# A depthwise convolution with silu, moved from the fused scan stage into the input projection

## What is computed

```
u = x @ W_in  -> [q | k | v | forget logits | z | xBC | dt | gate_att | gate_ssm]

def causal_conv(xbc, buf, w, b):
    xp = jnp.concatenate([buf.astype(xbc.dtype), xbc], axis=1)
    y = b
    for j in range(CONV_WIDTH):
        y = y + w[j] * xp[:, j:j + l]
    return jax.nn.silu(y), xp[:, l:]

def mamba_branch(z, xbc, ...):
    xbc, new_buf = causal_conv(xbc, conv_buf, conv_w, conv_b)
    xs, bm, cm = jnp.split(xbc, [D_SSM, D_SSM + SSM_GROUPS * SSM_STATE], axis=-1)
    ...                                    # chunked scan over xs, bm, cm; gate by silu(z); grouped norm
```

## Time and profile before

| | |
|---|---|
| median of 3 runs | 5410.88 us (5408.63 to 5411.28) |
| profiled execution | 5412.87 us, its span 5411.1 us |
| TensorE / VectorE / ScalarE / GpSimd busy in the span | 75% / 61% / 16% / 27% |
| projection | 0 to 1476 us, TensorE at its full clock |
| fused stage, groups 0 to 6 | 1532 to 2114 us |
| fused stage, last group | 2114 to 2192 us |
| merge and experts | 2192 to 5411 us |

### The profile page before, as it was taken

One profiled execution on the slowest core, in us unless ns is written; L12 is line 12 of the kernel. 1 busy time (PEld: TensorE's weight loads), 2 busy tenths in 40 slices (PEclk: granted clock), 3 DMA queues, 4 the chain that ended last, 5 costly groups with the idle time before them and its releaser, 6 DMA issues. The chain is left out here.

```text
span 5411.1 us, 60657 instructions
## 1 busy us (share of the span) xinstructions
PE 4053.6 (75%) x24165; PEld 3236.8 (60%) x24165; DVE 3325.7 (61%) x4454; ACT 849.1 (16%) x1210; POOL 1463.3 (27%) x1609
## 2 busy tenths in 40 slices
PE   9999999999957777899999999999999900000000
PEld 7999999999935545798798555555555500000000
DVE  2322222222257766433452897878879789999998
ACT  2212221212112222322352000000000000000000
POOL 0000000000043333000010122222222367777774
PEclk9999999999967777899999999999999955555555
DMA  4332323232177876534564999999999999999998
GB/s 156 117 126 100 106 100 105 100 106 100 57 254 271 289 278 241 196 110 169 173 211 161 355 419 419 398 418 421 421 420 419 421 379 410 410 410 409 410 410 331
DMA packets 336652, 1462.02 MB, mean 270 GB/s; under 512 B 84452, under 2 KB 113028, under 8 KB 196600
## 3 DMA queue, kind: packets, MB, share of 16 engines
q0 software_dynamic: 174304, 995.20, 46.1%
q1 hardware_dynamic: 131304, 430.86, 22.0%
q10 hardware_dynamic: 30768, 32.11, 1.8%
HBM read 1362.71 MB, written 94.75 MB: 269 GB/s over the span
## 5 line engine op out<-in xcount | busy, mean ns | idle before, releaser
L2231 DVE SCALAR_TENSOR_TENSOR i_acc<-i_row,i_cf,i_acc 128x2048 f32<-128x2048 f32 x571 | 1344.8, 2355 | 156.1 <-DMA i_row<-in_expert_v,i_ei 119.3
L2038 PE MATMUL i_p_h<-i_xT,i_ut 128*128 128x384 f32 x4096 | 1322.4, 486 | 0.0
L2038 PEld LDWEIGHTS i_p_h<-i_xT,i_ut 128*128 128x128 f32 x4096 | 779.1, 190 | 540.9 <-issue 0.6
L2347 POOL DMA_INDIRECT i_row<-in_expert_v,i_ei x576 | 544.9, 946 | 633.7 <-DVE i_acc L2231 512.2
L246 PE MATMUL a_acc<-a_xh,a_wh 128*128 128x288 f32 x3104 | 672.2, 298 | 18.1 <-DVE a_xl L466 13.4
L246 PE MATMUL a_acc<-a_xh,a_wl 128*128 128x288 f32 x3104 | 665.2, 296 | 0.0
L246 PE MATMUL a_acc<-a_xl,a_wh 128*128 128x288 f32 x3104 | 664.8, 296 | 0.0
L246 PEld LDWEIGHTS a_acc<-a_xh,a_wh 128*128 128x128 f32 x3104 | 499.2, 189 | 29.6 <-issue 26.0
L2222 DVE CUSTOM_DVE_ANT_0 i_row<-i_row,i_acc 128x2048 f32<-128x2048 f32 x192 | 433.5, 2286 | 125.1 <-DMA i_row<-in_expert_u,i_ei 123.3
L246 PEld LDWEIGHTS a_acc<-a_xl,a_wh 128*128 128x128 f32 x3104 | 500.4, 189 | 0.0
L246 PEld LDWEIGHTS a_acc<-a_xh,a_wl 128*128 128x128 f32 x3104 | 500.3, 189 | 0.0
(11 more groups left out here) (310 smaller groups left out, 5450.9 us busy)
## 6 DMA issues: line engine op xcount, KB each, us to landing
i_ut<-in_u_tiles SPq DMA_DIRECT2D x128, 1024.0 KB, 9.7
a_w<-in_w_in SPq DMA_DIRECT2D x97, 1024.0 KB, 4.8
f_w<-in_w_out SPq DMA_DIRECT2D x32, 1024.0 KB, 5.1
f_w<-in_w_query SPq DMA_DIRECT2D x32, 1024.0 KB, 5.2
tmp_uT<-a_out POOLq DMA_DIRECT2D x97, 288.0 KB, 2.4
tmp_Ha<-i_ho ACTq DMA_DIRECT2D x128, 192.0 KB, 9.2
f_w<-in_w_bs SPq DMA_DIRECT2D x16, 1024.0 KB, 4.9
c_csb<-tmp_cs SPq DMA_DIRECT2D x32, 288.0 KB, 5.8
```

Of the source, the lines that this page charges most:

```text
L2038: last = nc.tensor.matmul(p_h[:, e % 2, 0:ND], ut[:, e % RU, k * P:(k + 1) * P], xT[:, k, :], start=(k == 0), stop=(k == KT - 1))
L2231: v.scalar_tensor_tensor(acc, row[:, m % R, :], cf[:, j, k:k + 1], acc, ALU.mult, ALU.add).then_inc(row_used, 1)
L2347: pool.indirect_dma_start(row[:, m % R, :], None, table, bass.IndirectOffsetOnAxis(index, axis=0)).then_inc(row_in[m % R], 16)
```

## The change

The convolution and its silu are done in the projection, on the tile that was just evicted. The tiles get new places in `uT`: in each round of 20 slots, the 8 slots with t % 5 in (1, 3) compute tiles of `xBC`, the 12 others those of z and the gates. In a convolution slot VectorE runs `conv` right behind its eviction: 4 small copies and 8 arithmetic instructions, the same shapes as before. ScalarE does the silu in the slot after, in front of its eviction. GpSimd doesn't store the raw tile; it stores the finished one as `xcT` and the new convolution state (27 columns) as `convT`. SyncE loads the channels' taps, bias and old state (29 columns) along with each such tile's weights. The fused stage loads the finished tiles into `xc2`, and its edges, convolution and silu are gone.

```
--- before.py
+++ after.py
+    CONV = [t for t in range(SLOTS) if t % 5 in (1, 3)]
+    PLAIN = [t for t in range(SLOTS) if t % 5 not in (1, 3)]
...
+                    if t in CONV:
+                        c = CONV.index(t)
+                        if type(r) is not int or c >= 4:
+                            sp.wait_ge(conv_sum, 8 * r + c - 3)
+                        sp.dma_start(cp[:, c % 4, :], io["conv_par"][ds(8 * r + c, 1)].rearrange("a p n -> (a p) n")
+                                     ).then_inc(cp_in[c % 4], 16)
...
+                def silu(r, c):
+                    act.wait_ge(conv_sum, 8 * r + c + 1)
+                    nc.scalar.activation(cv[:, c % 2, :], cv[:, c % 2, :], ACT.Silu).then_inc(conv_out, 1)
...
+                    if t - 1 in CONV:
+                        silu(r, CONV.index(t - 1))
                     evict_late(r, t)
...
+                def conv(r, t):
+                    dve.drain()
+                    dve.wait_ge(copied_a, SLOTS * r + FIRST + t + 1)
+                    dve.wait_ge(cp_in[c % 4], 32 * r + 16 * (c // 4) + 16)
+                    if type(r) is not int or c >= 2:
+                        dve.wait_ge(x_stored, 8 * r + c - 1)
...
                     evict(FIRST + t, r)
+                    if t in CONV:
+                        conv(r, t)
...
+                    if late and tau - FIRST in CONV:
+                        pool.wait_ge(conv_sum, 8 * r + CONV.index(tau - FIRST) + 1)
+                        pool.sem_inc(stored[tau % RING], 16)
+                        return
...
+                def store_conv(r, c):
+                    pool.wait_ge(conv_out, 8 * r + c + 1)
...
+                    pool.wait_ge(x_flight, 32 * 8 * r + 32 * c + 32)
+                    pool.sem_inc(x_stored, 1)
...
-                        sp.wait_ge(conv_sum, 4 * g + 8)
-                        load_raw(g + 2)
+                        load_xc(g + 2)
...
-                    if g < 7:
-                        conv_edges(g + 1)
                     after_matrix(g, 0)
...
-                    if g < 7:
-                        conv(g + 1, 2)
                     after_matrix(g, 2)
...
-                    for i, a in enumerate((2, 3, 0, 1) if g else range(4)):
-                        act.wait_ge(conv_sum, 4 * g + i + 1)
-                        nc.scalar.activation(xc[:, a, :], xc[:, a, :], ACT.Silu).then_inc(conv_out, 1)
                     act.wait_ge(loaded[k], NLOAD * (g // 2) + NLOAD)
...
-                        pe.wait_ge(conv_out, 4 * g + 4)
+                        pe.wait_ge(xc_in[g % 2], 48 * (g // 2) + 48)
```

More of the change, by code:

```diff
@@ L166, in project_and_prompt @@
         mask = sb("d_mask", [P, P])
+        cv = sb("f_cv", [P, 2, T])
+        cp = sb("f_cp", [P, 4, 5 + 3 * NB])
+        samp = sb("f_samp", [P, NB, 3 + TB])
+        tail = sb("f_tail", [P, 2, 3 + 3 * NB])
+        cp_in = [tl.sem(f"f_cp_in{k}") for k in range(4)]
+        conv_sum = tl.sem("f_conv_sum")
+        conv_out = tl.sem("f_conv_out")
+        x_flight = tl.pool_sem("f_flight")
+        x_stored = tl.sem("f_stored")
         p_s, p_t, p_o = acc[:, 4:6, :], acc[:, 6, :], acc[:, 7, :]
@@ L226, in _, with body @@
                     load_tile(tau)
-                with sp.Fori(0, ROUNDS) as r:
-                    for t in range(SLOTS):
-                        it = FIRST + V_ITEMS + t
-                        sp.wait_ge(w_split, SLOTS * r + it - RING + 1)
-                        sp.dma_start(w[:, it % RING, :], io["w_in"][ds(SLOTS * r + FIRST + t, 1)].rearrange("a p k n -> (a p) (k n)")
-                                     ).then_inc(w_in[it % RING], 16)
+                def body(r, t):
+                    it = FIRST + V_ITEMS + t
+                    sp.wait_ge(w_split, SLOTS * r + it - RING + 1)
+                    sp.dma_start(w[:, it % RING, :], io["w_in"][ds(tile_of(r, t), 1)].rearrange("a p k n -> (a p) (k n)")
+                                 ).then_inc(w_in[it % RING], 16)
+                    if t in CONV:
[4 more added lines that the diff above has]
+                                     ).then_inc(cp_in[c % 4], 16)
+                rounds(sp, body)
             @block.tensor
@@ L560, in output @@
                     v.tensor_copy(o[:, k % 2, :], p_o[0:DH, :]).then_inc(o_out, 1)
+                def conv(r, t):
+                    c = CONV.index(t)
+                    slot = (FIRST + t) % RING
+                    raw, xc, par4 = out[:, slot, :], cv[:, c % 2, :], cp[:, c % 4, :]
+                    tap = lambda j: par4[:, j:j + 1]
+                    sv = xc[:, TP:T].rearrange("p (b t) -> p b t", t=TB)
+                    rv = raw[:, TP:T].rearrange("p (b t) -> p b t", t=TB)
+                    dve.drain()
[3 more added lines that the diff above has]
+                        dve.wait_ge(x_stored, 8 * r + c - 1)
+                    v.tensor_copy(samp[:, :, 0:3], par4[:, 5:5 + 3 * NB].rearrange("p (b c) -> p b c", c=3))
+                    v.tensor_copy(samp[:, :, 3:3 + TB], rv)
+                    v.tensor_copy(tail[:, c % 2, 0:3], raw[:, TP - 3:TP])
+                    v.tensor_copy(tail[:, c % 2, 3:3 + 3 * NB].rearrange("p (b c) -> p b c", c=3), rv[:, :, TB - 3:TB])
+                    v.tensor_scalar(xc[:, 0:TP], raw[:, 0:TP], tap(3), par4[:, 4:5], ALU.mult, ALU.add)
+                    dve.drain()
+                    v.tensor_scalar(sv, samp[:, :, 3:3 + TB], tap(3), par4[:, 4:5], ALU.mult, ALU.add)
+                    for j in range(3):
+                        i = 3 - j
+                        dve.drain()
+                        v.scalar_tensor_tensor(xc[:, i:TP], raw[:, 0:TP - i], tap(j), xc[:, i:TP], ALU.mult, ALU.add)
+                        last = v.scalar_tensor_tensor(sv, samp[:, :, j:j + TB], tap(j), sv, ALU.mult, ALU.add)
+                    last.then_inc(conv_sum, 1)
                 back = lambda r, s, n: (r, s - n) if s >= n else (r - 1, s - n + STEPS)
@@ L655, in mamba_and_samples @@
     FACN = 5 * 3 * SR
-    GC = 24
+    GC = 4
     RK, RV = 6, 4
@@ L669, in mamba_and_samples @@
         ones = sb("c_ones", [P, P])
-        raw = sb("c_raw", [P, 4, T])
-        old = sb("c_old", [P, 4, NB, 3])
         gc = sb("c_gc", [P, SG, GC])
@@ L728, in mamba_and_samples @@
         gc_in = tl.sem("c_gc_in")
-        raw_in = tl.sem("c_raw_in")
-        padded = tl.sem("c_padded")
-        conv_sum = tl.sem("c_conv_sum")
-        conv_out = tl.sem("c_conv_out")
+        xc_in = [tl.sem(f"c_xc_in{k}") for k in range(2)]
         exp_out = tl.sem("c_exp_out")
@@ L860, in _ @@
                         load_group(g + 2)
-                for s in (tail_st, h_st, s_st, m_st, att_st):
+                for s in (h_st, s_st, m_st, att_st):
                     sp.wait_ge(s, 128)
@@ L1087, in _ @@
                 dve.drain().then_inc(index_out, 1)
-                conv_edges(0)
-                dve.wait_ge(gc_in, 16)
-                for a in range(4):
-                    conv(0, a)
                 query(0)
@@ L1094, in _ @@
                 dve.wait_ge(const_in, 128)
+                dve.wait_ge(gc_in, 16)
                 for g in range(8):
@@ L1185, in _ @@
                     if g < 7:
-                        conv(g + 1)
+                        gate(g + 1)
                     act.wait_ge(l_out, g + 1)
@@ L2494 @@
     ssm_s = o["ssm_sT"].transpose(2, 0, 3, 1).reshape(1, NB, SH, 64, SN)
-    order = np.argsort(np.array([[2 * g, 2 * g + 1, 16 + g, 24 + g] for g in range(SG)]).ravel())
-    conv = o["convT"].reshape(SG, P, 4, 27).transpose(0, 2, 1, 3).reshape(32, P, 27)[order].reshape(4096, 27).T
+    conv = o["convT"].reshape(4096, 27).T
     c = np.ascontiguousarray
```

93 lines of the change are left out of this document (29 added, 64 removed).

## The result

| | before | after |
|---|---|---|
| median | 5410.79 us (4 runs) | 5338.42 us (5338.01 to 5347.52, 4 runs) |
| ratio, 95% interval | 1 | 0.9871 [0.9854, 0.9888] |
| span of the profiled execution | 5411.1 us | 5336.3 us |

The change makes the kernel 72 us faster; 5359 was forecast, with a range of 5338 to 5392. The time lies 0.4 us inside the lower end. The table shares out the 74.8 us between the two spans by the same three pieces of a group that the prediction uses, with one row more for the way into the stage. A length is read between VectorE's starts: of `e_sn` (group start), of the 1536-column reduction (maximum), of `c_z <- c_y, c_z` (gating).

What follows compares the result with a forecast made beforehand. TensorE was taken to bound the projection, a chain through several engines the fused stage. Gains of 6 + 11.2 + 34.5 = 51.7 us from 5410.88 gave 5359 us; range 5338 to 5392 with B and C.

Steps and rivals of the forecast that it cites:

- The added work: Projection: about 4.5 us of VectorE per convolution, 32 of 80 slots, hidden under TensorE's products; cost 0.
- Rival D: Projection: convolution overruns slots with t % 5 = 2, 16 times; at 13 us each, net 5434 us; chance 0.04.
- Step 1: Fused stage's start: VectorE's first four convolutions go, but it waits for forget values anyway; gain 0 us.
- Step 2: Group 0, first chunk: wait for `c_old` and edges go; gain 6 us, bounds 3.6 and 7.2.
- Step 3: Groups 1 to 6, start to maximum: edges worth 0, one convolution removed gains 1.87 us each, 11.2 us.
- rival B: TensorE's clock: first key products also faster, 10 us more, 5349 us; or low level stays, 5368 us; chance 0.21.
- Step 4: Maximum to gating, 38.08 us: the chain runs through value pages, not the two convolutions; gain 0 for 7 groups.
- Rival C: Fused stage: pages land later, 3 to 4 us per group go back, half the gain; 5385 us; chance 0.16.
- Step 5: Gating to next start: without the fourth silu `e_ov` runs earlier, ending TensorE's 3.67 us idle; gain 34.5 us.
- A: The forecast itself, whole kernel: 5359 us, own range 5350 to 5370 us; chance 0.55.

Runs made afterwards that it cites:

- The run with early drains: Kernel before, with one GpSimd drain added per projection round, ahead of the 19th slot's store, where it idles; 5401.53 us, ratio 0.9985 to the kernel before.
- The run with the load loop: Kernel before, with only SyncE's loop over the late tiles written as in the changed kernel (round 0 apart); 5409.54 us, ratio 1.0001 to the kernel before.
- 7 more operations: Changed kernel with seven more 576-column VectorE operations behind each of the projection's 32 convolutions; 5408.71 us, ratio 0.9996 to the kernel before.
- repeated run: The changed kernel itself, unaltered, run once more on the second chip; 5340.52 us, ratio 0.9868 to the kernel before.
- the run with the gap put back: Changed kernel with about 5 us of unused ScalarE copies ahead of `e_ov` in groups 0 to 6; 5431.4 us, ratio 0.9949 to the kernel before.

## Why the prediction was right, and where it was off

**The added work** costs nothing, as forecast. The convolution took 4.3 us where 4.5 was estimated, the margin behind it is 3.8 us as worked out, 2.6 us more fit into it and 6.2 us more don't. Rival D's break-even was put at 11.5 us per convolution. At 4.3 + 6.2 = 10.5 us the gain, by then 72 us instead of 51.7, was already gone: an overrun of 2.4 us costs 4.5 us per slot, since the products slow down as well. So D was nearer than it was made, though still far off at 4.3.

**Step 1, start of the stage,** is the one term that was missing. Its argument held: from the block's start to the start of group 0 are 33.9 us before (1498.35 to 1532.28) and 34.2 after (1490.99 to 1525.14), so removing VectorE's first convolutions gave nothing. But the block itself began 7.4 us earlier, since GpSimd's drain at the end of the projection fell from 9.87 to 3.09 us. The prediction counted GpSimd's new stores as hidden and didn't ask what they change at the block's end. The run with early drains shows that the drain can be moved: made 9.5 us shorter, it let the block start 7.8 us earlier. The run with the load loop excludes the other candidate. Why the change made the drain shorter isn't shown, so these 7 us came by luck.

**Step 2, group 0,** gave 9.9 us for 6, above its upper bound of 7.2. Start to first output fell by 8.1 us (19.71 to 11.62). Of it, 3.6 to 5.3 us are the wait for `c_old` and the edges, as forecast; the rest are key pages. Before, TensorE waited for one of them for 5.27 us in the first chunk, and after for 0.76 and 1.91 us:

```profile
1539.72 1.08 PE L1281 MATMUL e_ps<-e_kr,e_qp 128*32 128x128 f32 x16 [5.27 <-DMA e_kr<-in_cache_k,e_ik]
```

```profile
1528.08 1.08 PE L1292 MATMUL e_ps<-e_kr,e_qp 128*32 128x128 f32 x16 [0.76 <-DMA e_kr<-in_cache_k,e_ik]
...
1531.08 1.08 PE L1292 MATMUL e_ps<-e_kr,e_qp 128*32 128x128 f32 x16 [1.91 <-DMA e_kr<-in_cache_k,e_ik]
```

The traces show why. An issue of a key page takes GpSimd 0.94 us, but the one that runs beside VectorE's long scan takes 4 to 5 us. Before, this is the third key page, which starts 0.44 us behind the scan's start at 1525.57; after, the third had started 0.17 us ahead of the scan and it is the fourth:

```profile
1526.01 4.73 POOL L875 DMA_INDIRECT e_kr<-in_cache_k,e_ik  x1 [0.31 <-issue]
```

```profile
1518.43 4.42 DVE L1066 TENSOR_TENSOR_SCAN e_rev<-e_one,e_lf 128x2048 f32<-128x2048 f32 x1 [17.92 <-DMA e_lf<-in_cache_f,e_il]
1519.50 4.10 POOL L929 DMA_INDIRECT e_kr<-in_cache_k,e_ik  x1 [0.30 <-issue]
```

In two other runs of the changed stage (two convolutions put back, 7 more operations) the scan meets the third page, and there the first output comes 15.4 and 15.3 us after the start instead of 11.6. So some 4 of the 8.1 us hang on a few tenths of a microsecond, and are luck; the other 4 are the wait and the edges as forecast. By the maximum less is left of the difference: these two runs have 32.4 and 32.0 us for 30.7. So 8.4 us of the 9.9 came without that luck, still 1.2 above the upper bound, and what gave these isn't shown.

**Step 3, start to maximum,** gave 21.6 us for 11.2. Its own term was right: one convolution put back costs 1.9 us per group in groups 1 to 6, as the 1.87 said. What was missing is rival B's mechanism. From the group's start to the end of the first 64 key products TensorE needs 17.5 us over the six groups instead of 28.1, 10.7 less, about what the step lacks. In four of the six groups these key products take 1.95 us instead of 3.5 to 3.6; in the other two, groups 4 and 6, they still take 3.2, and in the repeated run again two others of the six are slow. What reaches the maximum is shown by the run with the gap put back, which has no convolutions either: the pause alone adds 6.6 us in groups 1 to 6 and 1.9 in group 7. So the clock, and not the missing convolutions, gave most of the missing 10 us; the rest, some 4 us, is what two traces of one kernel differ by, and isn't placed.

The edges were put at 0 because VectorE waits for TensorE there anyway. At the low clock that holds: with the gap put back and no edges the first output comes 7.5 us after the start, on average over groups 1 to 6, with the edges in the kernel before 7.2. In the changed kernel it comes after 6.2 us; whether the edges would still be free there wasn't tried.

**Step 4, maximum to gating,** gave 0.4 us for 0. Two convolutions put back there cost nothing that can be told, and value pages asked for earlier, with two more places for them, take 63 us off the same stretch. The chain runs through the value pages, as the earlier trace rows had said. Rival C, later pages, didn't come: DMA's share rose to 0.86 and the stretch kept its length.

**Step 5, gating to the next start,** gave 34.3 us for 34.5, with one error that another hid. Five of the seven take 7.31 us and not 8.05, since the turn and the new scores take 2.4 us at the higher clock where 2.99 had been read behind a pause. Group 4 took 10.93 and group 6 took 9.08; TensorE came to them at the lower clock, and the sums of squares ran at about half speed, here in group 4:

```profile
1886.93 2.29 PE L1266 MATMUL c_p_cb<-c_mo,c_ones 128*128 128x288 f32 x4
1889.01 2.13 PE L1266 MATMUL c_p_s<-c_mo,c_ones 128*128 128x288 f32 x4
```

They take 1.24 and 1.13 us in the group shown above. By which groups are hit the sum moves: 56.6 us here and 63.3 in the repeated run.

**The rivals.** A's mechanism was whole, but its own range of 5350 to 5370 was left; B, given 0.21, came out beside it, at about the 10 us that it named. With B's 10 us A is at 5349, and the drain's 7 and group 0's 4 us make 5338. That the wide range still holds is in part luck: its lower end of 5338 counted 10 us of faster products in step 4, which gave 0.4, and it held by 0.4 us because the drain and group 0 gave 11 us that the sum didn't have. The rule quoted with B, from the Trainium skill's "TensorE: Matmul & The Clock Gate" (Why this matters for your kernels), that idle gaps between bursts of matmuls bring the half clock, agrees with the trace of before in six of seven groups (0.69 us for the turn behind 3.67 us of idle time) and with the run that put the gap back (0.69 us behind 3.41 us, 0.38 without). It should have had more than a fifth of the chance: the prediction saw both durations behind the same gap and took that for indecision, where the shorter turn stood in one group of seven, and even there the key products behind it took 3.64 us.

The rule of "DMA: Bandwidth & Descriptors" (Specifications) against short rows, 116 and 108 B here, changed nothing that a run shows. The state's stores landed in 4.8 us (median), where 15.1 had been read the earlier trace rows; nothing was late for them, and no run shows what short rows cost by themselves.

## What to carry to other kernels

Work moved under a stage that TensorE bounds is free only up to the margin of its tightest slot; beyond it a slot costs more than the overrun, here 4.5 us for 2.5, because the products behind each wait slow down too. When an edit closes a pause of TensorE's, read the matmuls behind the pause at both of their durations and give the faster one to what follows without a gap a price of its own. And look at each engine's last instruction at the end of a block: what an engine has to clear there is paid by all of them, and can be paid earlier in idle time.

## What the runs showed of the hardware

With few stores since the last drain, GpSimd's drain lasts 0.05 us and 0.082 us for each of them (4 stores 0.38, 8 stores 0.70, 24 stores 2.01, 32 stores 2.66, 55 stores 4.56, 59 stores 4.88 us), though all these stores had landed. Without drains between, 131 stores gave 9.87 and 163 gave 3.09 us, the same to the nanosecond in each trace of its kind; by the line they would have been 10.8 and 13.4.

A pause of TensorE's of 3.4 to 3.7 us at the end of a group was followed by new scores at half speed (3.42 for 1.85 us) in six of seven groups, and by key products at half speed (3.5 to 3.6 for 1.95 us) in all seven. In the two traces of the changed kernel, without the pause, the new scores are at half speed in none and in one of seven groups, and the key products slow (3.2 to 3.6 us) in three and in two.

An issue of an indirect page by GpSimd took 0.94 us, and 3.96 to 5.11 us in each of the 14 traces where it ran beside VectorE's scan of 2048 columns (4.42 us); the next issue took 2.1 us.
